# The recurrence's gate products as three rounded products each, with widened small blocks, in a two-block transformer kernel

## The reference

```python
def rg_lru(x, w_a, b_a, w_x, b_x, lam):
    xb = x.reshape(bsz, s, RNN_BLOCKS, RNN_BLOCK_W)                     # 16 blocks of 84 channels
    r = jax.nn.sigmoid(jnp.einsum('bsnc,ncd->bsnd', xb, w_a).reshape(bsz, s, D_RNN) + b_a)
    i = jax.nn.sigmoid(jnp.einsum('bsnc,ncd->bsnd', xb, w_x).reshape(bsz, s, D_RNN) + b_x)
    log_a = LRU_C * r * jax.nn.log_sigmoid(lam)
    a = jnp.exp(log_a)
    u = jnp.sqrt(-jnp.expm1(2.0 * log_a)) * (i * x)
```

## Time and profile before

| | |
|---|---|
| median of 3 runs | 812.32 us (812.21 to 812.46) |
| span of the profiled execution, first to last instruction | 810.6 us |
| outside the span (median less span) | 1.7 us |
| PE busy | 799.6 us, 99% of the span |
| DVE busy | 599.4 us, 74% |
| ACT busy | 487.0 us, 60% |
| POOL busy | 27.1 us, 3% |
| granted TensorE clock, mean | 0.998 |

### The profile page before, as it was taken

One profiled execution on the slowest core, in us unless ns is written; L12 is line 12 of the kernel. 1 busy time (PEld: TensorE's weight loads), 2 busy tenths in 40 slices (PEclk: granted clock), 3 DMA queues, 4 the chain that ended last, 5 costly groups with the idle time before them and its releaser, 6 DMA issues.

```text
span 810.6 us, 11913 instructions
## 1 busy us (share of the span) xinstructions
PE 799.6 (99%) x4813; PEld 693.2 (86%) x4813; DVE 599.4 (74%) x773; ACT 487.0 (60%) x738; POOL 27.1 (3%) x38
## 2 busy tenths in 40 slices
PE   8999999999999999999999999999999999999996
PEld 7889998888888888988888888888888988888885
DVE  6774698998957986897878778877777665655556
ACT  6555598877757454765666566546755654544552
POOL 1102000000000000000000000020110000000000
PEclk9999999999999999999999999999999999999999
DMA  8446432342434674456455555764453655555441
GB/s 337 164 156 251 170 126 104 118 155 73 151 119 159 229 288 156 156 188 227 160 206 174 201 197 175 256 237 147 146 196 121 211 201 196 174 219 191 161 152 52
DMA packets 22630, 143.79 MB, mean 177 GB/s; under 512 B 2608, under 2 KB 3248, under 8 KB 8240
## 3 DMA queue, kind: packets, MB, share of 16 engines
q1 hardware_dynamic: 20880, 137.72, 48.3%
q10 hardware_dynamic: 1696, 5.31, 1.8%
HBM read 141.97 MB, written 1.05 MB: 176 GB/s over the span
## 4 chain that ended last, share of the span: by engine, by line
PE 93%; ACT 3%; DVE 2%; DMA 1%; issue 1%; DVEq 0%; SPq 0%; ACTq 0%
PE PS L1748 19%; PE PS L1752 10%; PE PS L1801 10%; PE PS L1802 10%; PE PS L1805 10%; PE PS L1735 5%; PE PS L1736 4%; PE PS L1740 4%; PE PS L2115 3%; PE PS L1764 2%; PE PS L2094 2%; PE PS L1858 1%; PE PS L1892 1%; PE PS L2119 1%; PE PS L1869 1%; PE PS L2065 1%
## 5 line engine op out<-in xcount | busy, mean ns | idle before, releaser
L1074 DVE TENSOR_TENSOR WL<-RAW,WH 128x2048 fp32r<-128x2048 f32 (+2 forms) x127 | 285.1, 2247 | 31.1 <-ACT WH L629 31.0
L629 ACT ACTIVATE WH<-RAW 128x2048 fp32r<-128x2048 f32 (+2 forms) x127 | 238.2, 1877 | 47.0 <-PE PS L1805 25.7
L1490 DVE TENSOR_TENSOR HLS<-PS,HLS 128x512 f32<-128x512 f32 x46 | 31.7, 689 | 92.7 <-ACT HLS L977 92.7
L1748 PE MATMUL PS<-CHL,WH 128*128 128x512 f32 x352 | 87.9, 392 | 0.0
L1735 PE MATMUL PS<-BHL,WH 128*126 128x256 f32 (+1 forms) x336 | 83.6, 287 | 0.0
L977 ACT ACTIVATE HLS<-PS 128x512 f32<-128x512 f32 x46 | 27.4, 595 | 90.7 <-PE PS L1752 86.3
L1736 PE MATMUL PS<-BHL,WH 128*126 128x256 f32 (+1 forms) x336 | 81.8, 282 | 0.0
L1748 PE MATMUL PS<-BHL,WH 128*128 128x512 f32 x320 | 79.9, 392 | 0.0
L1748 PEld LDWEIGHTS PS<-CHL,WH 128*128 128x128 f32 x352 | 63.9, 189 | 11.8
L1802 PE MATMUL PS<-WH,AHL 128*128 128x512 f32 x176 | 68.8, 391 | 0.0
L1801 PE MATMUL PS<-WH,AHL 128*128 128x512 f32 x176 | 68.7, 390 | 0.0
(11 more groups left out here) (313 smaller groups left out, 1311.1 us busy)
## 6 DMA issues: line engine op xcount, KB each, us to landing
RAW<-in_w_stream SPq DMA_DIRECT2D x108, 1024.0 KB, 4.8
RAW<-in_w_stream SPq DMA_DIRECT2D x11, 1008.0 KB, 4.9
RAW<-in_w_stream SPq DMA_DIRECT2D x8, 704.0 KB, 4.5
WF<-in_w_stream SPq DMA_DIRECT2D x2, 1024.0 KB, 5.4
LN<-in_ln ACTq DMA_DIRECT2D x2, 1024.0 KB, 5.2
WF<-in_w_stream SPq DMA_DIRECT2D x4, 294.0 KB, 3.6
X<-in_x SPq DMA_DIRECT2D x2, 512.0 KB, 4.2
RAW<-in_w_stream SPq DMA_DIRECT2D x2, 512.0 KB, 6.8
```

Of the source, the lines that this page charges most:

```text
L629: eng.activation(WH[:, c % NSLOT, 0:CHUNKS[c][2]], raw(c), ACT.Copy).then_inc(w_hi, 1)
L1074: eng.tensor_tensor(WL[:, c % NSLOT, 0:CHUNKS[c][2]], raw(c), f32(WH[:, c % NSLOT, 0:CHUNKS[c][2]]), ALU.subtract).then_inc(w_lo, 1)
L1490: eng.tensor_tensor(HLS[:, n % 4, :, :], PS[:, bank:bank + 2, 0:TOK], HLS[:, n % 4, :, :], ALU.add)\
L1748: eng.matmul(PS[:, bank, :], wh, HL[:, k, :, :].rearrange("p a t -> p (a t)"), start=(k == 0), stop=False)
```

## The change

1. The chunks `ri` become split chunks: loaded into `RAW`, rounded by ACT into `WH`, subtracted by DVE into `WL`. They now take part in the rotation of the two `RAW` slots. Their widths grow from 588 (840 in group 1) to 716 (968) columns, because the small blocks are padded with zero columns.
2. The convolved tiles of a group are rounded by ACT (`rg_round`, in the pass right after the last `rnn` chunk, behind `unit_exp` and ahead of `side`) and the remainder is taken by POOL, in one instruction for each group.
3. PE forms each gate product as three products of rounded parts. It waits for POOL's remainder ahead of all of them. The four small products of a group become twelve, with 42 rows of weights as before, but 106 columns, of which 64 are zero; they write PSUM rows 0 to 105.
4. Four semaphores of the second feed-forward part are merged with those of the first; the waits stay the same.

```diff
 def gate_cols(g):
-    return RG_TILES[g] * RP + HB
+    return RG_TILES[g] * RP + 64 + HB
...
-        out += [("ri", g, 2 * gate_cols(g), False)]
+        out += [("ri", g, 2 * gate_cols(g), True)]
...
+RNN_LAST = [max(c for c in range(AT["ri", g]) if CHUNKS[c][0] == "rnn") for g in range(NG)]
...
(POOL)
+            for G in range(NG):
+                tiles = slice(RG_AT[G], RG_AT[G + 1])
+                eng.wait_ge(xc_hi, G + 1)
+                eng.tensor_tensor(AL[0:RP, tiles, :], XC[:, G % 2, 0:RG_TILES[G], :], f32(AH[0:RP, tiles, :]), ALU.subtract)\
+                   .then_inc(xc_lo, 1)
...
(ACT)
+            def rg_round(G):
+                eng.wait_ge(mb_dve, RNN_THROUGH[G])
+                eng.activation(AH[0:RP, RG_AT[G]:RG_AT[G + 1], :], XC[:, G % 2, 0:RG_TILES[G], :], ACT.Copy).then_inc(xc_hi, 1)
...
+                if c - 1 in RNN_LAST:
+                    rg_round(RNN_LAST.index(c - 1))
                 side(c)
...
(PE)
                     eng.wait_ge(mb_dve, RNN_THROUGH[i])
-                    w = plain(c).rearrange("p (a n) -> p a n", a=2)
+                    eng.wait_ge(xc_lo, i + 1)
+                    wh, wl = (W[:, c % NSLOT, 0:2 * gate_cols(i)].rearrange("p (a n) -> p a n", a=2) for W in (WH, WL))
...
                         for which in range(2):
-                            last = eng.matmul(PS[0:RP, banks[t], 256 * which:256 * which + 256],
-                                              w[0:RP, which, RP * t:RP * t + RP], XC[:, i % 2, t, :], start=(which == 0),
+                            rows = wh[0:RP, which, RP * t:RP * t + RP]
+                            eng.matmul(outs[which], rows, AH[0:RP, k, :], start=(which == 0), stop=False, skip_group_check=True)
+                            eng.matmul(outs[which], rows, AL[0:RP, k, :], start=False, stop=False, skip_group_check=True)
+                        if m == 0:
+                            eng.wait_ge(w_lo, SPLIT_NO[c] + 1)
+                        for which in range(2):
+                            last = eng.matmul(outs[which], wl[0:RP, which, RP * t:RP * t + RP], AH[0:RP, k, :], start=False,
                                               stop=(t == 2), skip_group_check=True)
...
+                        for n, (W, A) in enumerate(((wh, AH), (wh, AL), (wl, AH))):
+                            other = W[:, which, RP * RG_TILES[i]:gate_cols(i)]
+                            ins = eng.matmul(PS[0:64 + HB, banks[0], cols], other[0:HB, 0:64 + HB], A[0:HB, first + 1, :],
+                                             start=False, stop=(which == 1 and n == 2), skip_group_check=True)
+                            last = eng.matmul(PS[0:64 + HB, banks[1], cols], other[64:64 + HB, 0:64 + HB], A[64:64 + HB, first, :],
+                                              start=False, stop=(which == 1 and n == 2), skip_group_check=True)
```

More of the change, by code:

```diff
@@ L453, in two_block_program @@
             "mix_done", "os_ready", "os_ss", "os_rstd", "mr_ready", "mrt_done", "mrt_hi", "mrt_lo"))
[L454 to L458, removed]
+        y_mean, y_std, eps_ready, x0_low, y_ln, xt4_done, xt4_hi, xt4_lo = (sem(n) for n in (
+            "y_mean", "y_std", "eps_ready", "x0_low", "y_ln", "xt4_done", "xt4_hi", "xt4_lo"))
+        z_gain, wt_ready, rnn_in, xw_ready, gate_t_done, x_sq2 = (sem(n) for n in (
+            "z_gain", "wt_ready", "rnn_in", "xw_ready", "gate_t_done", "x_sq2"))
+        half_copied, halves_summed, xc_hi, xc_lo = (sem(n) for n in ("half_copied", "halves_summed", "xc_hi", "xc_lo"))
         def wait_tile(eng, c, t):
@@ L975, in half_copy @@
                 if n >= 4:
-                    eng.wait_ge(up_conv if n - 4 < N_UP else up2_prod, n - 3 if n - 4 < N_UP else n - 3 - N_UP)
+                    eng.wait_ge(up_conv if n - 4 < N_UP else up_prod, n - 3)
                 eng.activation(HLS[:, n % 4, :, :], PS[:, bank:bank + 2, TOK:2 * TOK], ACT.Copy).then_inc(half_copied, 1)
@@ L2069, in main @@
                             last.then_inc(ri_part, 1)
+                    first = RG_AT[i]
                     for which in range(2):
                         cols = slice(256 * which, 256 * which + 256)
-                        other = w[:, which, RP * RG_TILES[i]:gate_cols(i)]
-                        ins = eng.matmul(PS[64:64 + HB, banks[0], cols], other[0:HB], XC[0:HB, i % 2, 1, :],
-                                         start=False, stop=(which == 1), skip_group_check=True)
-                        last = eng.matmul(PS[0:HB, banks[1], cols], other[64:64 + HB], XC[64:64 + HB, i % 2, 0, :],
-                                          start=False, stop=(which == 1), skip_group_check=True)
+                        for n, (W, A) in enumerate(((wh, AH), (wh, AL), (wl, AH))):
[4 more added lines that the diff above has]
+                                              start=False, stop=(which == 1 and n == 2), skip_group_check=True)
                     ins.then_inc(ri_part, 1)
@@ L2152, in main @@
                 if kind in ("dn", "dn2"):
-                    first_bank, lo_s, n_all = (2, up_lo, N_UP // 2) if kind == "dn" else (0, up2_lo, N_UP2 // 2)
+                    first_bank, before, n_all = (2, 0, N_UP // 2) if kind == "dn" else (0, N_UP, N_UP2 // 2)
                     def down_half(cc, j, t, n):
@@ L2158, in down_half @@
                                       j == 0, j == n_all - 1)
-                    eng.wait_ge(lo_s, 2 * i + 2)
+                    eng.wait_ge(up_lo, before + 2 * i + 2)
                     if i < n_all - 2:
@@ L2171, in main @@
                         eng.wait_ge(w_hi, SPLIT_NO[c + 1] + 1)
-                        eng.wait_ge(lo_s, 2 * i + 3)
-                        eng.wait_ge(up_hi if kind == "dn" else up2_hi, 2 * i + 4)
+                        eng.wait_ge(up_lo, before + 2 * i + 3)
+                        eng.wait_ge(up_hi, before + 2 * i + 4)
                         s = (c + 1) % NSLOT
@@ L2188, in main @@
                             eng.matmul(outs[n], AH[:, units[1], 0:P], weights(WL, 1, n), start=False, stop=False)
-                        eng.wait_ge(lo_s, 2 * i + 4)
+                        eng.wait_ge(up_lo, before + 2 * i + 4)
                         for n in range(2):
@@ L2414, in gates_blocks @@
             first, second = rows_of[0, 64:64 + HB], rows_of[1, 0:HB]
-            out[0:HB, which, n * RP:] = dense[second[:, None], first[None, :]]
-            out[64:64 + HB, which, n * RP:] = dense[first[:, None], second[None, :]]
+            out[0:HB, which, n * RP + 64:] = dense[second[:, None], first[None, :]]
+            out[64:64 + HB, which, n * RP:n * RP + HB] = dense[first[:, None], second[None, :]]
         return out.reshape(P, -1)
```

18 lines of the change are left out of this document (10 added, 8 removed).

## The result

The changed kernel takes 820.84 us (median; 820.21 to 823.29), the kernel before 812.30 us (812.21 to 812.46). The ratio is 1.0110, with a 95% interval of 1.0098 to 1.0122. Slower was right, but the forecast of 817.6 us was about 3.2 us too low. The measured time lies above the forecast's own range of 816 to 819.5 us and near the upper end of the wider one (813.8 to 821.2), close to the 820.6 us of the rival in which the clock falls. The profiled execution of the changed kernel took 821.1 us, with a span of 819.4, so its extra is 8.8 us.

The account below looks back on a forecast made before the run. PE, busy 99% of the span, was taken as the bound, so its stalls are paid in full. Terms of -0.5 + 3.9 + 1.5 + 0.85 - 0.5 = +5.25 us gave 817.6 us, own range 816 to 819.5, wider 813.8 to 821.2.

Parts of the forecast that it names:

- The clock rival: Group 1: the clock falls in the 4.5 us stall, gate products behind it take twice as long, +3.0, 820.6 us; chance 0.14.
- if PE's busy share stays what it is elsewhere: Condition on the forecast of 817.6 us: PE stays as busy outside the places counted as it was before.
- the prediction's own signs of being wrong: Group 1's gates within 2 us of the transposes ahead, ACT or DVE slack unseen in waits, or a granted clock drop.
- the sum of +5.25: Whole kernel: -0.5 + 3.9 + 1.5 + 0.85 - 0.5 us over the five groups, giving a span of 815.9 us.
- Group 1, 4.5 us of stall: Group 1's gates: PE waits 4.5 us for POOL, ending at 127.0; less 0.6 for the products, +3.9.
- Group 2, +1.5: Group 2: no stall at the gates; POOL's subtraction slows DVE, whose late copy of unit 3 delays the transposes, +1.5 us.
- Group 3, +0.85: Group 3: chunk 30's split and the rounding make the gates 1.35 us late, less 0.5 for the products.
- Groups 0 and 4, -0.5: Groups 0 and 4: rounding and split fit into ACT's idle time, so each gains 0.5 us from the products.
- Single file: Every group's small products run one after another, 0.71 us more each, mostly hidden in group 2; +2.8, 820.4 us; chance 0.10.
- Half of the stalls: Group 1 stalls 2.8 us instead of 4.5 and group 2's copy is in time (-1.0): 814.9 us; chance 0.13.
- The bare chain: Group 1: only rounding, POOL and hand-over behind exponentials ending as now cost 2.8 us; 812.2 us, no change; chance 0.06.
- The gain alone: All groups: ACT and POOL finish before PE comes, leaving only the products' 2.9 us gain; 809.4 us; chance 0.05.

Follow-up runs that it names:

- experiment 1: Changed kernel with 20 extra 128x512 matmuls, results overwritten, ahead of PE's wait for POOL at group 1's gates: 818.90 us, ratio 1.0079.
- experiment 6: Changed kernel with the gate products of the kernel before and unsplit gate weights, keeping the rounding, subtraction and PE's wait: 818.78 us, ratio 1.0074.
- experiment 9: Kernel before with only the new form of gate products, on long-ready parts of the normalised input, part of the computation left out: 810.70 us, ratio 0.9979.
- experiment 5: Changed kernel without rounding, subtraction and PE's wait, products reading another long-ready activation, weights' split kept: 814.02 us, ratio 1.0031.
- experiment 2: Changed kernel with ACT's rounding of the convolved tiles put ahead of a unit's exponentials: 814.39 us, ratio 1.0029.
- experiment 4: Changed kernel with a group's twelve small products reordered, six on one row half first, then six on the other: 822.50 us, ratio 1.0126.
- experiment 10: The change in groups 0 and 4 only, groups 1 to 3 as in the kernel before: 811.69 us beside 812.39, ratio 0.9992.
- experiment 3: Changed kernel with the rounding first in ACT's pass and the gate weights split at the pass's end on ACT and DVE: 816.19 us, ratio 1.0045.
- experiment 7: On top of experiment 2, the merge tile's tanh in group 1 also ahead of unit 2's exponentials: 816.26 us, ratio 1.0050.

## What the prediction had right, and the step that failed

**The step that failed** is the condition of the sum, "if PE's busy share stays what it is elsewhere", which also stands for the clock: with it the sum puts the fall of the clock at nothing. It fell in the stall of group 1 and cost 1.9 us in the gates behind it (experiment 1). The clock rival had 0.14; it is what happened, and a falling clock is one of the prediction's own signs of being wrong. The rival's place was right (the gates of group 1), its size 3.0 us, measured 1.9.

The changed kernel's span is 3.55 us longer than the sum of +5.25. By the table, 2.07 of them are in group 1 and vanish when its wait is filled. The others are small: 0.6 in group 1 without the clock, 0.25 and 0.32 in groups 2 and 3, 0.1 in groups 0 and 4, and 0.22 behind them.

I had the row that speaks for it, and had a stall of 4.5 us in my own sum. The row was read a little short. PE's last matmul of the kernel before stands on its timeline as

```profile
802.77 0.61 PE L1805 MATMUL PS<-WL,AHL 128*128 128x512 f32 x2
```

so PE had been idle for 3.3 us when the clock fell, not for 2.6. That is still less than 4.5. To hold 0.52 for "the clock stays" against that was the error: the rival was a consequence of the forecast, not an alternative to it.

**Group 1, 4.5 us of stall: right to 0.3.** I had POOL's end at 127.0; it was 126.78, and PE started at 127.03, having arrived 0.47 us earlier through group 0. The chain ahead ran 0.4 us earlier than I said. POOL lost most of that again: it took 2.15 us where I had 1.9. It started at 124.63 beside DVE's scan, which ended at 125.19, and 1.6 us after that it was done; DVE's product behind the scan (125.22) took 2.11 us instead of 0.69. From POOL's end to PE's start another 0.25 us passed. The bare chain without the weights' split I had at 2.8 us; experiment 6 has 2.95. The gain of 0.6 on the products was 0.33 (experiment 1) to 0.4 (experiment 9), since ACT frees the third bank no faster.

**Group 2, +1.5: +1.75, but not by the way I gave.** I said POOL would keep its 1.3 us and end before PE comes. POOL's timeline has:

```profile
95.42 2.85 POOL L598 TENSOR_TENSOR AHL<-XC,AHL 126x512 fp32r<-126x512 f32 x1 [14.34 <-ACT AHL L666]
...
166.95 2.31 POOL L598 TENSOR_TENSOR AHL<-XC,AHL 126x512 fp32r<-126x512 f32 x1 [40.18 <-ACT AHL L666]
...
209.56 1.30 POOL L598 TENSOR_TENSOR AHL<-XC,AHL 126x512 fp32r<-126x512 f32 x1 [40.30 <-ACT AHL L666]
```

and DVE's timeline beside it:

```profile
165.85 2.28 DVE L1086 TENSOR_TENSOR WL<-RAW,WH 128x2048 fp32r<-128x2048 f32 x1
168.06 2.82 DVE L1159 TENSOR_TENSOR_SCAN XC<-AA,XC 126x768 f32<-126x768 f32 x1
```

At 166.95 POOL runs 1.0 us longer than at its shortest (1.30) and ends 1.13 us after DVE's split does, at 168.13; DVE's scan, 1.75 us in experiment 5, takes 1.07 more. Both pay, each for the other's instruction that was there first. DVE's 1.0 to 1.1 us was right; "POOL kept its 1.295", read from the one place in the earlier trace rows, was not a rule. The result is a stall of 0.92 us ahead of the gates, where I had none "by a hair", and 0.55 ahead of the transposes.

The Trainium skill (GPSIMD Engine Reference, Specifications) says that the two engines contend for SBUF interfaces where DVE has two SBUF inputs. The rows agree, and in these places they fit two engines that take turns, an instruction at a time, with GpSimd waiting as well as DVE: POOL ended 1.13 us after DVE's split in group 2, and 1.15 us after it in group 0, where the split ran to 97.12. The estimates worked out from the same page of the Trainium skill (Performance versus the Vector engine), 1.1 and 1.7 us, lie near the 1.13 and 1.6 us that POOL took once DVE was done, and near the 1.30 and 1.82 us of experiment 2.

**Group 3, +0.85: +1.17.** 0.59 at unit 9's scores (forecast 0.5), 1.04 more at the gates, and 0.46 back. **Groups 0 and 4, -0.5: -0.47 and -0.43**, and gates in 2.38 us where I had 2.28. In group 0 that was close: POOL took 2.85 us and was done at 98.27, not at 96.9, half a microsecond before PE came.

**Single file** (0.10) did not happen, and in experiment 4, where the halves still overlapped in part, it cost 0.15 to 0.33 us a group, not 0.71. **Half of the stalls** (814.9 us) has nearly the time of experiment 2 (814.39). **The bare chain** has the stall of experiment 6 (2.8 and 2.95 us), not its time, which is 818.78 with the fallen clock and without the gain of the products. **The gain alone**, 2.9 us by my upper bound, is 1.7 when nothing stands in its way (experiment 9): the 2.9 ignored what waits in group 1 and just behind group 2.

## What to carry to other kernels

Where PE is busy 99% of the time, price a change by what it queues ahead of the engines that feed PE: here 1.7 us of shorter products came with some 3 us for splitting their weights (experiments 5 and 9), and 6.5 us for rounding behind the exponentials and waiting for POOL, the fallen clock included (experiment 6). If a forecast contains a stall of PE that is longer than one after which the trace already shows the clock down, put the clock into the sum, not among the rivals. And a wait that is removed often shows the next one a few tenths behind it (banks freed by ACT in group 1, DVE's copy in group 2); apply such a change only in the groups with idle time in front, as in experiment 10.

## What the runs showed of the hardware

- Much shorter idle stretches than 4.8 us can cost the clock. In experiment 3 the longest idle piece of PE was 1.78 us, ended at 125.30; the granted clock was 0.86 from 124 to 126 and 0.50 in the next window. In experiment 7 the pieces were 0.78 and 1.84 us, and it fell too. In the profiled execution of experiment 2, with pieces of 0.79, 0.70 and 0.25 us, it stayed at 1.00, and so it did in that of experiment 5, with 1.38 and 0.25.
- It differs between executions of the same kernel: of the seven of experiment 5, five had a mean clock of 0.997 to 0.999 and took 813.5 to 814.6 us, two had 0.994 and took 816.8 and 816.9. Experiment 2 has nine at 814.0 to 814.6 and two at 816.8 and 817.5, with 0.994. In experiment 6, with a stall of 2.95 us, it is three against two.
- How long the low level lasts varies as well. Worked out from the means of the windows, it lasted until some 128.8 us in experiment 3, until 132.5 in the changed kernel and until 139.4 in experiment 4, from a start between 125.4 and 125.8 in all three.
- At the low level passes of 256 columns started 0.213 us apart instead of 0.118: 1.8 times, not 2.
